# The last two blocks of every expert stream, taken out of the guarded loop into fixed rounds

## The reference

```python
def hier_moe(h, w_rg, b_rg, w_re, b_re, w1, w3, w2):     # cut
    ...                                                   # 2 experts and 2 gates per token
    def run(args):
        xb, e = args
        return (jax.nn.silu(xb @ w1[e]) * (xb @ w3[e])) @ w2[e]
    ys = lax.map(run, (xs, block_e)).reshape(-1, d_)
    return jnp.zeros_like(h).at[slot_tok].add(ys * slot_gate[:, None])
```

```
layer 0  stream 0, 15 blocks  N r N r N r N N N N N N N N r
         stream 1, 14 blocks  N N N r N r N N N N N r N N
         stream 2, 11 blocks  N N r N N N N N N N N
layer 1  stream 0, 15 blocks  N N N N r N r r r N N N N N N
         stream 1, 12 blocks  N N N N r N N N N N N N
         stream 2, 16 blocks  N N N r N r r r r r N N N N N N
```

## Time and profile before

| | us |
|---|---|
| median of three runs | 3165.96 |
| the three runs | 3165.96, 3169.25, 3161.48 |
| the profiled execution | 3160.6 |
| its span in the profile | 3158.8 |
| expert stage of layer 0: first product to last output | 1572.3 to 2137.8 |
| expert stage of layer 1: first product to last output | 2521.8 to 3111.0 |

### The profile page before, as it was taken

One profiled execution on the slowest core, in us unless ns is written; L12 is line 12 of the kernel. 1 busy time (PEld: TensorE's weight loads), 2 busy tenths in 40 slices (PEclk: granted clock), 3 DMA queues, 4 the chain that ended last, 5 costly groups with the idle time before them and its releaser, 6 DMA issues.

```text
span 3158.8 us, 33588 instructions
## 1 busy us (share of the span) xinstructions
PE 2755.3 (87%) x11408; PEld 1258.6 (40%) x11408; DVE 1079.2 (34%) x2096; ACT 457.9 (14%) x846; POOL 320.9 (10%) x446
## 2 busy tenths in 40 slices
PE   6999969999998999999599978873999688999773
PEld 3444424444444446564533322222555433333221
DVE  3998960330003042454531111117244521111114
ACT  2111132100011010540100100001052100011000
POOL 0101012000000000000122211110000221222110
PEclk9999989999999999999599999986999699999886
DMA  6655521211220311000789999965100699779993
GB/s 214 205 189 193 173 107 55 96 64 69 80 80 0 117 54 49 5 12 31 262 329 373 380 393 393 389 240 194 56 26 23 240 359 382 277 264 364 392 373 134
DMA packets 272211, 603.02 MB, mean 191 GB/s; under 512 B 18437, under 2 KB 43333, under 8 KB 272001
## 3 DMA queue, kind: packets, MB, share of 16 engines
q1 hardware_dynamic: 256864, 580.70, 50.5%
q0 software_dynamic: 15264, 21.24, 1.9%
HBM read 743.04 MB, written 29.20 MB: 244 GB/s over the span
## 4 chain that ended last, share of the span: by engine, by line
PE 69%; SPq 12%; DMA 7%; DVE 6%; issue 3%; ACT 2%; POOL 0%; POOLq 0%; DVEq 0%; ACTq 0%
PE psum L1309 11%; PE psum L969 11%; PE psum L1018 10%; SPq L620 10%; PE psum L1146 9%; PE psum L990 7%; DMA arena<-in_w 5%; PE psum L1331 4%; PE psum L1241 4%; PE psum L1193 2%; PE psum L1182 1%; PE psum L954 1%; PE psum L1039 1%; PE psum L1256 1%; PE psum L1205 1%
## 5 line engine op out<-in xcount | busy, mean ns | idle before, releaser
L1309 PE MATMUL psum<-arena 128*64 128x512 f32 x2656 | 647.3, 633 | 117.3 <-DMA arena<-in_w 115.7
L1309 PEld LDWEIGHTS psum<-arena 128*64 128x64 f32 x2656 | 196.0, 144 | 448.4 <-issue 443.2
L969 PE MATMUL psum<-arena 128*128 128x512 f32 x768 | 344.1, 601 | 2.8 <-ACT arena L700 2.8
L1018 PE MATMUL psum<-arena 128*128 128x512 f32 x768 | 329.9, 592 | 0.8 <-ACT arena L692 0.8
L1406 DVE SCALAR_TENSOR_TENSOR arena<-arena 128x512 f32<-128x512 f32 x464 | 308.7, 745 | 0.0
L1331 PE MATMUL psum<-arena 128*64 128x512 f32 x1328 | 301.9, 598 | 0.0
L1146 PE MATMUL psum<-arena 128*128 128x512 f32 (+1 forms) x800 | 288.9, 523 | 5.9 <-issue 4.0
L990 PE MATMUL psum<-arena 128*128 128x512 f32 x512 | 225.3, 603 | 11.1 <-POOL arena L2049 10.4
L1018 PEld LDWEIGHTS psum<-arena 128*128 128x128 f32 x768 | 145.8, 190 | 184.2 <-issue 183.2
L969 PEld LDWEIGHTS psum<-arena 128*128 128x128 f32 x768 | 142.5, 190 | 174.2 <-issue 174.2
L1146 PEld LDWEIGHTS psum<-arena 128*128 128x128 f32 x800 | 153.2, 193 | 134.7 <-issue 125.0
(11 more groups left out here) (269 smaller groups left out, 2123.5 us busy)
## 6 DMA issues: line engine op xcount, KB each, us to landing
arena<-in_w SPq DMA_DIRECT2D x261, 2048.0 KB
arena<-in_w_ada SPq DMA_DIRECT2D x48, 1024.0 KB, 5.2
arena<-in_conv_w_in SPq DMA_DIRECT2D x24, 1024.0 KB
arena<-in_ret_w_in SPq DMA_DIRECT2D x12, 2048.0 KB, 8.1
arena<-in_w_in SPq DMA_DIRECT2D x8, 2048.0 KB, 8.3
arena<-moe_out SPq DMA_DIRECT2D x10, 1024.0 KB, 9.8
arena<-in_conv_w_out SPq DMA_DIRECT2D x4, 2048.0 KB, 10.3
arena<-in_ret_w_out SPq DMA_DIRECT2D x4, 2048.0 KB, 7.7
```

Of the source, the lines that this page charges most:

```text
L969: m = pe.matmul(bank(b + c), w[:, k, c * P:(c + 1) * P], c_hT[:, k, :], start=(k == 0), stop=(k == KD - 1))
L1018: m = pe.matmul(bank(4 * (n % 2) + j), l_, r_, start=(k == 0), stop=(k == KD - 1))
L1309: m = pe.matmul(bank(2 * s)[part], m_xsT[s][:, at:at + SB], m_w[s][j][:, k, :], start=(k == 0), stop=(k == KD - 1))
```

## The change

`rounds` runs the loop with all three streams only up to round 7, and the guarded loop from round 8 up to the third block from the end of each stream (`i < n[s]`, where `n[s]` is the stream's number of blocks less two). As many rounds of the guarded loop are passed over as before. After it every engine has two more rounds written out, each with all three streams: blocks n[s], then blocks n[s]+1. So a shorter stream no longer ends earlier; its last two blocks wait until the longest has two left. In the last round there are no steps for a further block (no gather, no turn of rows, no w1 and w3), and TensorE's outputs of a stream's last block follow the next stream's products; the turn of its hidden rows stands in the middle of these products.

```diff
-            with eng.Fori(first, E // NS) as i:
+            with eng.Fori(first, E // NS - 2) as i:
                 for s in range(NS):
                     step(s, i, first)
...
+            with eng.Fori(E // NS - 2, NBS[l] - 2) as i:
+                with eng.If(i < n[NS]):
+                    for s in range(NS):
+                        with eng.If(i < n[s]):
+                            step(s, i, first)
@@ SyncE
-                rounds(sp, l, last, load_step)
+                rounds(sp, l, n, load_step)
+                for s in range(NS):
+                    load_step(s, n[s], 2)
+                for s in range(NS):
+                    e, new = expert(s, n[s] + 1)
+                    sp.wait_ge(moe(l, s, "out"), count(l, s, "out", n[s] + 1))
+                    weights(s, 2, "w2", e, new)
@@ ScalarE
                 for s in range(NS):
-                    outputs_copied(s, last[s], 1)
+                    silu_step(s, n[s], 2)
+                for s in range(NS):
+                    silu_step(s, n[s] + 1, 2)
+                    if s >= 1:
+                        outputs_copied(s - 1, n[s - 1] + 1, 1)
+                outputs_copied(NS - 1, n[NS - 1] + 1, 1)
@@ TensorE
                         if k == KD // 2 and early >= 1:
                             turn_hidden(s, i - 1, early - 1)
+                        if k == KD // 2 and also is not None:
+                            turn_hidden(also, n[also] + 1, 1)
...
                 for s in range(NS):
-                    turn_hidden(s, last[s], 1)
+                    expert_step(s, n[s], 2)
                 for s in range(NS):
-                    outputs(s, last[s], 1)
+                    products(s, n[s] + 1, 2, s - 1 if s >= 1 else None)
+                    outputs(s, n[s], 1)
+                    if s >= 1:
+                        outputs(s - 1, n[s - 1] + 1, 1)
+                turn_hidden(NS - 1, n[NS - 1] + 1, 1)
+                outputs(NS - 1, n[NS - 1] + 1, 1)
@@ VectorE
                 for s in range(NS):
-                    hidden_copied(s, last[s], 1)
+                    gate_step(s, n[s], 2)
+                for s in range(NS):
+                    hidden_copied(s, n[s], 1)
+                    if s >= 1:
+                        hidden_copied(s - 1, n[s - 1] + 1, 1)
+                    gated(s, n[s] + 1, 2)
+                hidden_copied(NS - 1, n[NS - 1] + 1, 1)
@@ GpSimd
                 for s in range(NS):
-                    scatter(s, last[s], 1, 2 * last[s] + 4)
+                    scatter(s, n[s] - 1, 1, 2 * n[s] + 2)
                 for s in range(NS):
+                    scatter(s, n[s], 1, 2 * n[s] + 3)
+                    if s >= 1:
+                        scatter(s - 1, n[s - 1] + 1, 1, 2 * n[s - 1] + 4)
+                scatter(NS - 1, n[NS - 1] + 1, 1, 2 * n[NS - 1] + 4)
```

More of the change, by code:

```diff
@@ L68, in blocks_per_stream @@
 def blocks_per_stream(n):
-    loop = E // NS
-    return loop + GROUP * (-(-(EPN + 2 * n // SB - loop) // GROUP))
+    return EPN + 2 * n // SB
 V_CW, V_LNG, V_LNB, V_CN, V_RN, V_C, V_SC, V_GB = 0, 512, 528, 544, 552, 560, 576, 588
@@ L426, in count, with rounds @@
             return shared(l, s, what)[1] + n
-        def rounds(eng, l, last, step, first=2):
+        def rounds(eng, l, n, step, first=2):
             for i in range(first):
@@ L432, in rounds, with blocks_but_two @@
                     step(s, i, i)
-            with eng.Fori(first, E // NS) as i:
+            with eng.Fori(first, E // NS - 2) as i:
                 for s in range(NS):
                     step(s, i, first)
[L436 to L447, removed]
+            with eng.Fori(E // NS - 2, NBS[l] - 2) as i:
[3 more added lines that the diff above has]
+                            step(s, i, first)
+        def blocks_but_two(eng, l):
+            return [eng.value_load(g_n[l][0:1, s:s + 1], min_val=E // NS - 4, max_val=NBS[l] - 4) + 2
                     for s in range(NS + 1)]
@@ L615, in _ @@
                 first_weights(2, 1)
-                last = last_blocks(sp, l)
+                n = blocks_but_two(sp, l)
                 def weights(s, j, what, e, new):
@@ L641, in load_step @@
                         weights(s, 2, "w2", e, new)
-                rounds(sp, l, last, load_step)
+                rounds(sp, l, n, load_step)
[5 more added lines that the diff above has]
+                    weights(s, 2, "w2", e, new)
                 sp.wait_ge(sem("fin_x"), past_full(2 * l + 1) + nt)
-                sp.wait_ge(moe(l, 2, "product"), count(l, 2, "product", last[2] + 1))
+                sp.wait_ge(moe(l, 2, "product"), count(l, 2, "product", n[2] + 2))
                 sp.sem_inc(sem("settled"), 1)
-                sp.wait_ge(moe(l, 2, "w13"), count(l, 2, "w13", 32 * last[2] + 64))
+                sp.wait_ge(moe(l, 2, "w13"), count(l, 2, "w13", 32 * n[2] + 64))
                 sp.sem_inc(sem("settled"), 1)
@@ L650, in _ @@
                     mod_row(l, who, 5, who)
-                sp.wait_ge(moe(l, 2, "out"), count(l, 2, "out", last[2] + 1))
+                sp.wait_ge(moe(l, 2, "out"), count(l, 2, "out", n[2] + 2))
                 sp.sem_inc(sem("settled"), 1)
@@ L655, in _ @@
                 for s in range(2):
-                    sp.wait_ge(moe(l, s, "w13"), count(l, s, "w13", 32 * last[s] + 64))
+                    sp.wait_ge(moe(l, s, "w13"), count(l, s, "w13", 32 * n[s] + 64))
                     sp.sem_inc(sem("settled"), 1)
@@ L892, in _ @@
                 act.wait_ge(sem("meta"), past("meta", l) + 1)
-                last = last_blocks(act, l)
+                n = blocks_but_two(act, l)
                 def outputs_copied(s, i, early):
@@ L909, in silu_step @@
                         outputs_copied(s, i - 1, early - 1)
-                rounds(act, l, last, silu_step)
+                rounds(act, l, n, silu_step)
                 for s in range(NS):
-                    outputs_copied(s, last[s], 1)
+                    silu_step(s, n[s], 2)
[4 more added lines that the diff above has]
+                outputs_copied(NS - 1, n[NS - 1] + 1, 1)
                 for i_ in range(nt):
@@ L1286, in _ @@
                 pe.wait_ge(sem("meta"), past("meta", l) + 1)
-                last = last_blocks(pe, l)
+                n = blocks_but_two(pe, l)
                 def turn_rows(s, i, early):
@@ L1297, in turn_rows, with products @@
                     m.then_inc(moe(l, s, "turned"), 1)
-                def products(s, i, early):
+                def products(s, i, early, also=None):
                     pe.wait_ge(moe(l, s, "w13"), count(l, s, "w13", 32 * i + 32))
@@ L1345, in _ @@
                 turn_rows(0, 0, 0)
-                rounds(pe, l, last, expert_step)
+                rounds(pe, l, n, expert_step)
                 for s in range(NS):
-                    turn_hidden(s, last[s], 1)
+                    expert_step(s, n[s], 2)
                 for s in range(NS):
-                    outputs(s, last[s], 1)
+                    products(s, n[s] + 1, 2, s - 1 if s >= 1 else None)
[4 more added lines that the diff above has]
+                outputs(NS - 1, n[NS - 1] + 1, 1)
         @block.vector
@@ L1931, in _ @@
                     end = NS * (EPN - 1) + s
-                    link(dve.tensor_scalar(be[0:1, s:s + 1], pend[0:1, end:end + 1], -float(stream_row(l, s) + 2), None,
+                    link(dve.tensor_scalar(be[0:1, s:s + 1], pend[0:1, end:end + 1], -float(stream_row(l, s) + 4), None,
                                            ALU.add))
@@ L1950, in _ @@
                 link(dve.tensor_copy(g_slot_gate[:, 0:nr], bank(5, nr, 256)[0:SB]))
-                last = last_blocks(dve, l)
+                n = blocks_but_two(dve, l)
                 def rows_copied(s, i, early):
@@ L1967, in hidden_copied, with gated @@
                         .then_inc(moe(l, s, "hid_rows"), 1)
-                def gate_step(s, i, early):
-                    if early >= 1:
-                        hidden_copied(s, i - 1, early - 1)
+                def gated(s, i, early):
                     row = i + stream_row(l, s)
@@ L1977, in gate_step @@
                                              op0=ALU.mult, op1=ALU.mult).then_inc(moe(l, s, "hidden"), 1)
+                def gate_step(s, i, early):
+                    if early >= 1:
+                        hidden_copied(s, i - 1, early - 1)
+                    gated(s, i, early)
                     if early == 0 and s + 1 < NS:
@@ L1993, in _ @@
                 rows_copied(0, 0, 0)
-                rounds(dve, l, last, gate_step)
+                rounds(dve, l, n, gate_step)
                 for s in range(NS):
-                    hidden_copied(s, last[s], 1)
+                    gate_step(s, n[s], 2)
[5 more added lines that the diff above has]
+                hidden_copied(NS - 1, n[NS - 1] + 1, 1)
                 dve.wait_ge(sem("mod_in"), past("mod_in", l) + 64 * (2 - l))
@@ L2120, in _ @@
                 pool.wait_ge(sem("meta"), past("meta", l) + 1)
```

(15 more changed lines are left out.)

1 line of the change is left out of this document (removed).

## The result

| | before | after |
|---|---|---|
| median, 12 runs each | 3162.66 us | 3171.59 us |
| lowest and highest | 3157.94, 3169.25 | 3167.24, 3175.69 |
| span of the profiled execution | 3158.8 | 3168.1 |

The change makes the kernel 8.9 us slower: the ratio is 1.0028, with a 95% interval of 1.0020 to 1.0035. So it is slower clear of the noise, by just less than the 0.3% up to which the prediction spoke of "same"; the interval goes over that edge. The forecast was 3.2 us slower.

What follows compares the result with a forecast made beforehand. Weight loads set the pace in the two expert stages, with passed rounds and three outputs bare behind the last weights. Layer 0 at 3.7 less and layer 1 at 6.9 more gave +3.2, so 3169 us, range 3152 to 3188.

Steps and rivals of the forecast that it cites:

- The place of the passing: Passed rounds before 0/13: layer 0's 20 hidden behind weights landing at 2047.6, layer 1's 11 bare, ending at 3020.4.
- The replay of block starts: Both expert stages: each moved block's start summed from measured paces, 11.6 us a block on TensorE, about 5.5 a weight unit.
- The new wait: Layer 1, before the outputs of 0/14: their w2, sent later behind other loads, lands at 3089.1, a wait of 9.3 us.
- last outputs 4 us earlier in layer 0, 7 later in layer 1: Trace sign at each stage's end, counted from its first product; the layer sums were 3.7 less and 6.9 more.
- The restart of the outputs of 0/14: Layer 1, after the wait for w2: a slow TensorE restart adding 1.7 us, so these outputs end at 3094.3.
- one price of 2.2 after over 10 us of idle: TensorE in both layers: a restart after such idle costs 2.2 us, 5.9 for the first 16 matmuls against 3.65.
- the faster rival: End of both layers: moved loads follow without a gap, ending 21 and 11 us earlier, 3134 us; chance 0.09.
- The slower one: Passed rounds in both layers: under a full DMA each costs twice as much, adding 12.5 and 6.5, 3188 us; chance 0.17.
- The third: Layer 1: w2 of 0/14 overtakes loads ahead of it, so 9.3 and 1.7 vanish, 3158 us; chance 0.12.
- The dummies: Both layers: three dummy-row turns each, six gathers and three row copies removed beside other work; 83 copies and gathers remain.

Runs made afterwards that it cites:

- e2_after_no_pass: The change with the guarded loop bounded at this run's own longest stream (13 and 14 rounds), so no round is passed over: 3166.5 us, ratio 1.0015.
- e1_old_tail: The change with the order of its last round undone, so last hidden rows and last outputs come after all three products: 3146.9 us, ratio 0.9948 to before.
- e5_no_last_w2: The change without loading each stream's last w2; last outputs use the w2 of the block before, so needed work is missing: 3145.1 us, ratio 0.9938.
- e10_after_pass_twice: The change with a second guarded loop of 20 and 11 rounds, all passed over, behind the first: 3177.9 us, ratio 1.0043 to before.
- e7_old_tail_dyn: e1_old_tail with the guarded loop's end read from the streams' lengths at run time: 3144.8 us, ratio 0.9947 to before.

## Why the prediction was right, and where its sizes were off

**The place of the passing** was right. In layer 0 it is hidden behind the weights of 0/13 (forecast 2047.6, measured 2048.36), and e2_after_no_pass shows that it costs nothing there. In layer 1 it is bare (forecast 0/13 at 3020.4, measured 3020.86), yet taking it away gives 4.1 us only.

**The replay of block starts** held for all moved blocks, within some 1 us:

| start of | forecast | measured |
|---|---|---|
| 0/10 in layer 0 | 1962.5 | 1962.3 |
| 0/13 in layer 0 | 2047.6 | 2048.4 |
| 2/10 in layer 0 | 2110.5 | 2111.0 |
| last outputs, layer 0 | 2130.5 | 2130.7 |
| 2/10 in layer 1 | 2906.5 | 2905.9 |
| 2/13 in layer 1 | 3000.0 | 2999.8 |
| 1/11 in layer 1 | 3068.3 | 3069.2 |
| outputs of 0/14, layer 1 | 3089.1 | 3089.2 |
| last outputs, layer 1 | 3114.3 | 3115.3 |

**The new wait** for the w2 of 0/14 was forecast at 9.3 and is 8.8; e1_old_tail and e5_no_last_w2 show that it and the two waits for the last w2 are the cost of the change. The prediction has these waits in its times (9.3, and by its own landings 5.0 and 3.5 before the last outputs, though it later says "about 3"; measured 4.9 and 4.6). What it did not say is their weight: in a sum near zero they and their restarts are some 25 us that hide a gain of 15. Its check "last outputs 4 us earlier in layer 0, 7 later in layer 1" came out as 0.2 earlier and 10.0 later.

**The terms that were mis-sized** are the slow restarts behind the waits. The last outputs were put at 3.6 us in both layers and took 5.95 and 5.20: 2.35 and 1.6 more. The restart of the outputs of 0/14 was put at 1.7 and is 2.7 (6.26 less 3.6), and everything behind them is as much later. Layer 1 is off by 3.1 us: 1.6 and 1.0 from these two restarts, and 0.5 because its stage began 0.5 us earlier in this execution while the weights did not come earlier. Layer 0 is off by 3.5: 2.35 from the restart, 0.9 from a stage that began 0.9 us earlier, and 0.2 because the last outputs start that much later than forecast.

The trace of the kernel before already had rows against one price of 2.2 after over 10 us of idle. A wait as long as the one of the earlier trace rows was followed by 5.34 and not 5.87, and one of 4.7 us by 6.50:

```profile
2989.39 5.34 PE L1309 MATMUL psum<-arena 128*64 128x512 f32 x16 [10.82 <-DMA arena<-in_w]
...
3038.25 6.50 PE L1309 MATMUL psum<-arena 128*64 128x512 f32 x16 [4.71 <-DMA arena<-in_w]
```

**What was luck.** The forecast time of 3169.2 is only 2.4 us below the measured 3171.6, but the change itself was forecast 5.7 too small (3.2 for 8.9). The rest cancels: the forecast stands on a median of three runs, 3166.0, and that of twelve is 3162.7, 3.3 lower. And with a change of 0.28% the outcome lies within the prediction's 0.3% by a hair; twelve runs of each kernel tell such a change from none.

**The rivals.** The weights do run dry (share 0.18 at 3003 to 3014), so the faster rival is out. The slower one is out by the 6.49 us of layer 1 and by e10_after_pass_twice. The third is out by the wait of 8.8 us: w2 of 0/14 landed 18.3 us after its send, behind the loads sent ahead of it, where a w2 alone takes 8.1, so it did not overtake them.

**The dummies** went as said: 83 row copies and 83 gathers, for 89 and 95. What that alone is worth was not measured.

**Left open**: what sets the price of a passed round (0.36 to 0.70), and what decides how slowly TensorE restarts; these restarts account for 2.7 of the 5 us by which layer 1 differs between two executions of the same work, the rest is open. The fixed rounds' loss of 9 us in layer 0 comes from one placement of this input's experts; other inputs were not tried.

## What to carry to other kernels

When a step is moved in front of another, look at the buffer that it needs. Outputs in front of the next stream's products are early for TensorE, but their weights are sent only when the outputs before them free the single buffer; they land 8 to 9 us later if sent alone (8.1 in the change, 8.9 in e1_old_tail) and 18 behind other loads, and everything after them stands. Work that waits for a late load belongs behind work that waits for nothing. And before hiding a cost ask whether it must be there: 20 us went away with a loop end read at run time, and with that in place the rearrangement was worth nothing on this input (3144.8 against 3141.8).

## What the runs showed of the hardware that was not expected

TensorE's restart after a wait is not one price, and it does not follow the length of the wait. The first 16 matmuls, 3.6 us at full clock, took 5.20 after a wait of 4.9 us and 5.95 after 4.6 in the change, and 6.50 after 4.7 before. After 10.6 to 10.8 us they took 5.8 in the change, 5.87 and 5.34 before. After 21.5 us they took 6.5 to 6.6 in the change and 5.0 in e7_old_tail_dyn. After some waits of 3.0 to 3.3 us they ran at 3.65 with no loss, after others of the same length at 5.35, in the same stage.

What it does follow is the granted clock of these matmuls. Windows of the kernel before: the wait and the first 16 matmuls of the block at 2950.5, the same of the block at 2966.9, and the first 16 of the block at 3038.2.

```profile
2947.30:2950.50 3.20, 0.06 (x1) 0.00 (x0) 0.69 (x1) 0.20 (x1) 1.43 (x3) 1.00 1.04 407
2950.50:2955.80 5.30, 5.27 (x16) 1.75 (x16) 0.00 (x0) 0.00 (x0) 1.02 (x1) 0.68 1.04 389
2963.80:2966.90 3.10, 0.08 (x1) 0.02 (x1) 0.69 (x1) 0.23 (x1) 1.43 (x3) 1.00 1.03 406
2966.90:2970.50 3.60, 3.59 (x17) 1.25 (x17) 0.00 (x0) 0.00 (x0) 1.03 (x1) 1.00 1.03 403
3038.20:3044.70 6.50, 6.45 (x17) 1.96 (x17) 0.00 (x0) 0.00 (x0) 0.00 (x0) 0.55 1.05 388
```

At a mean clock of 0.68, 3.65 us at full clock become 5.4 (measured 5.35), at 0.55 they become 6.6 (measured 6.50). With the two levels of 2.4 and 1.2 GHz a mean of 0.55 is nearly all at 1.2, one of 0.68 a part at each. After the first wait the clock fell only during the products; over the 16.4 us stand of the change's layer 0 it already is 0.64. So a slow restart is a time at the lower level that reaches into the products; why it follows one wait of 3.2 us and not another, no run here shows.

A passed round has no one price either: 0.70 and 0.60 us on TensorE in the first copy of the loop, and in a second copy behind it, by the difference worked out above, 0.36. It has to be measured where it stands.
